# Output sums of an older attention head inside the next key strip, norm roots read from PSUM, and a later release of weight strips 2 and 3

## Chip, cores and metric

The kernel runs on one core of one Trainium2 chip. The metric is the device time of one execution in microseconds, as the median of the runs. An engine is named by its role: TensorE (PE in the profile, PEld for its weight loads), VectorE (DVE), ScalarE (ACT), GpSimd (POOL), SyncE (SP).

## What is computed

Two diffusion blocks in a row on 256 latent tokens (x) and 256 context tokens (ctx) of width 2048, batch 1, all in fp32. Each block has two layers. A layer first normalizes both streams and modulates them with vectors that come from the conditions c and c_ctx, runs a mixer, and adds the gated result.

```python
h_lat = rms_norm(x, norm_g[i]) * (1.0 + scale[:, None]) + shift[:, None]
h_ctx = rms_norm(ctx, norm_g[i]) * (1.0 + cscale) + cshift
# block 1, layer 0: gated linear recurrence (rglru_mixer), both streams
# block 1, layer 1: differential attention, 16 heads of 2 x 64, latent queries, 512 keys
attn = p[:, :, 0] - lam * p[:, :, 1]          # two softmaxes per head
o = rms_norm(o, subln_g) * (1.0 - lam_init)   # over the 128 output features of a head
y_lat = (o * jax.nn.silu(g)) @ w_out
# block 2, layers 0 and 1: chunked SGU and grouped-query attention
x = x + gate[:, None] * y_lat
```

## The kernel before

**Layout and strips.** Activations lie with features on the 128 partitions, 16 tiles of 128 features, with 256 latent and 256 context tokens in the free dimension (512 together). Every projection is cut into strips: a strip is 128 output columns of a weight matrix, 128 x 2048, streamed from HBM in two halves of 512 KB. To keep fp32 precision at the fast matmul rate, weights and activations are split in a high and a low part (type fp32r). ScalarE writes the high part `w_hi` (`split_hi`, L223) and VectorE the rest `w_lo` (`split_lo`, L231), always one pair of strips ahead. TensorE makes three matmuls per feature tile (`strip`, L249 to L251), so a strip has two halves of 24 matmuls; `between(half)` is called after each half. SyncE issues the strip loads (`load_strip`, L215) and waits before each for the split of the strip two before it. Strips 0 and 1 are loaded at once, the loop over the other pairs begins behind a wait for `mod_used`, which counts products of modulation chunks (L1979).

**The start.** `start_pe` computes the first 8 groups of modulation columns. A group is four chunks of 1 MB, each multiplied with the conditions (`mod_products`, L299, 8 instructions as counted in the profile). GpSimd issues the chunk loads, chunk q of a group as soon as chunk q of the group before has been used (L1807). `mod_turn` (L322) turns a group's rows into columns, VectorE adds the bias and modulates four feature tiles, and TensorE runs the tiles of strips 0 and 1 that are ready (`first_tiles`, L288 to L290). The tiles 8 to 15 follow behind group 7.

**The norms.** `norm_pe` sums the squares into bank 6 (L484), ScalarE takes the root (L499), VectorE the reciprocal (L507), and TensorE broadcasts it over the partitions into the same bank (L493, semaphore `rstd_ps`). ScalarE copies it to SBUF (L503, `rstd_done`). VectorE, which in between has split half a strip, then multiplies tile by tile (`context`, L541 and L543), ScalarE adds the shift and writes the high part (L522), VectorE writes the low part (L550), and TensorE starts the tile in the next projection. There are four norms; the one in the start (layer 0) uses the copy in its own code.

**The attention.** `att_pe`, `att_act` and `att_dve` run one body per head i, in an order written by hand. `here` is the projection of head i: four strips, key (c = 0, 512 columns), query (1, 256), value (2, 512) and gate (3, 256). `before` is the attention of head i - 1, `older` the norm of the output of head i - 2. The queues of the engines are in order, with semaphores of one count per head between them. TensorE's body is: key strip, modulation chunk, scores of the head before (L1099), sum of squares of the older output (L1104, into bank 6, `M_BANK`), query strip, sum of squares of the keys (L1114, `M_BANK`), value strip, modulation chunk, sum of squares of the queries (L1118, `M_BANK`), transposes of the attention weights, gate strip, output product, value transposes. ScalarE copies and squares the keys (L1165, L1166), splits, takes the four exponentials (L1174), the root of the older sums (L1178), copies and squares the queries (L1183, L1184), splits, takes the root of the key sums (L1187), copies the values (L1191), and so on, with a tanh for the gate (L1207) and, at the end, the copy and square of the output (L1216, L1217, `o_evac`) and the copy of the turned values (L1223). VectorE uses the older root in `root()` (L1258 on) and the exponentials in `weights()` (L1268 to L1272). The sum, root and wait for an older head stand beside a head's own projection in the heads 2 to 15. The wait in question on TensorE is:

```python
                    pe.wait_ge(A["k_evac"], i + 1)
                    if older:
                        pe.wait_ge(A["sdo"], i - 1)
                    if before:
                        pe.wait_ge(A["sdq"], i)
                    pe.matmul(psum[:, M_BANK, :], ones64, ksq, start=True, stop=True).then_inc(A["ssk"], 1)
```

Of the kernel before, what the change touches and what calls it, by code (L numbers as in the profile page):

```python
# [22 lines left out]
ALU = mybir.AluOpType  # L23
ACT = mybir.ActivationFunctionType
AX_X = mybir.AxisListType.X

P = 128
D = 2048
KT = D // P
T = 256  # L30
NT = 2 * T
# [5 lines left out]
HEADS1 = 16  # L37
# [46 lines left out]
def build(nc, ins, out):  # L84
    with ExitStack() as ctx:
# [411 lines left out]
        def norm_sqrt(act, l):  # L497
            act.wait_ge(S["ss_done"], l + 1)
            act.activation(rcol, psum[:, SS_BANK, 0:NT // P], ACT.Sqrt, scale=1.0 / D, bias=eps_col).then_inc(S["sd_done"], 1)  # L499
            if l > 0:  # L500
                split_hi(act, layer_strip[l] // 2, 1, halves=(0,))
            act.wait_ge(S["rstd_ps"], l + 1)
            act.activation(nb["rstd"], psum[:, SS_BANK, :], ACT.Copy).then_inc(S["rstd_done"], 1)  # L503

# [25 lines left out]
        def norm_dve(dve, l):  # L530
# [4 lines left out]
            dve.wait_ge(S["unit_cols"], UNITS_READY[l])  # L535
            dve.wait_ge(S["rstd_done"], l + 1)
            dve.wait_ge(S["strip_done"], layer_strip[l])

            def context(k, c):
                dve.wait_ge(S["h_ready"], KT * l + k - 3)  # L540
                dve.scalar_tensor_tensor(out=hs4[c][:, 0:T], in0=xl[:, k, :], scalar=mod_a[:, bass.ds(k, 1), 0],  # L541
                                         in1=nb["rstd"][:, 0:T], op0=ALU.mult, op1=ALU.mult)
                dve.scalar_tensor_tensor(out=hs4[c][:, T:NT], in0=y[:, 1, k, :], scalar=mod_a[:, bass.ds(k, 1), 1],  # L543
                                         in1=nb["rstd"][:, T:NT], op0=ALU.mult, op1=ALU.mult).then_inc(S["hf_done"], 1)

# [472 lines left out]
        def att_strip(j, par, c):  # L1018
            return Strip(S_ATT, 4 * par + c, j, 8)
# [54 lines left out]
        def att_pe(pe):  # L1074
            def body(j, par):
# [3 lines left out]
                def chunk(n):  # L1079
                    return lambda half: mod_chunk(pe, M_ATT + j, 2 * par + n) if half else None  # L1080
                first = isinstance(i, int) and i == 0
                last, end = (isinstance(i, int) and i == HEADS1 + n for n in range(2))
                if first:
                    first_pair(pe, S_ATT, [(psum[:, K_BANK, :], NT), (psum[:, Q_BANK, 0:T], T)], KT, 0, KT)
                    chunk(0)(1)
                elif here:
                    ge(pe, A["v_evac"], i)
                    strip(pe, att_strip(j, par, 0), psum[:, K_BANK, :], NT, chunk(0))
                if before:
# [6 lines left out]
                    for qt in range(2):  # L1096
# [4 lines left out]
                        mm.then_inc(A["scores"], 1)  # L1101
                if older:
                    pe.wait_ge(A["o_evac"], i - 1)
                    pe.matmul(psum[:, M_BANK, 0:T], ones, osq, start=True, stop=True).then_inc(A["sso"], 1)  # L1104
                if here:
# [48 lines left out]
        def att_act(act):  # L1154
            def body(j, par):
# [3 lines left out]
                if last:  # L1159
                    to_high(act, 1, 0, 6)  # L1160
                if here:
                    st = att_strip(j, par, 0)
# [5 lines left out]
                if before:  # L1168
                    ge(act, A["attn_t"], 2 * (i - 1))
                    for qt in range(2):  # L1170
                        act.wait_ge(A["negmax"], 2 * (i - 1) + qt + 1)
                        for c in range(2):
                            n = 2 * qt + c
                            act.activation(p1[qt][c], psum[:, S_BANK + n, :], ACT.Exp, bias=nm1[:, n:n + 1],  # L1174
                                           accum_out=rs1[:, n:n + 1]).then_inc(A["expd"], 1)
                if older:
                    act.wait_ge(A["sso"], i - 1)
                    act.activation(osq, psum[:, M_BANK, 0:T], ACT.Sqrt, scale=1.0 / P, bias=eps_col).then_inc(A["sdo"], 1)  # L1178
                if here:
# [791 lines left out]
        def _(sp):  # L1971
# [4 lines left out]
            for par in range(2):  # L1976
                load_strip(sp, 0, par, True)
            sp.wait_ge(S["mod_used"], 4 * (MOD_FIRST - 2))
            with sp.Fori(1, N_STRIPS // 2) as pair:  # L1979
# [199 lines left out]
```

## Time and profile before

| | us |
|---|---|
| Median of 3 runs | 2805.18 (2803.17 to 2805.68) |
| Profiled execution, time | 2805.79 |
| Profiled execution, span | 2804.1 |
| TensorE busy in the span | 2639.0 |
| VectorE busy | 2045.8 |
| ScalarE busy | 1224.6 |

The span is what the profiler saw of one execution; the device time holds 1.7 us more around it. A busy time is the sum over an engine's instructions. Matmuls are pipelined, so the interval between two starts is shorter than the duration of one, and this text counts with starts.

### The profile page before, as it was taken

The numbers are of one execution on the slowest core, as the hardware profiler recorded it, in microseconds if no ns is written. First come the engines' busy times: TensorE is split into PE (matmuls) and PEld (weight loads), VectorE is DVE, ScalarE is ACT, GpSimd is POOL, SyncE is SP. The second block draws the span as 40 slices with busy tenths as digits, with TensorE's granted clock in tenths as the row PEclk, the third lists the DMA queues.
The fourth block names the chain that finished last, engine by engine and source line by source line (L and its number), as shares of the span: only waits on it lengthen the run. The fifth ranks groups of instructions, "written<-read, shape, count | busy, mean of one in ns | idle before, by whom it ended". The sixth has DMA issues, their size and how long they took to land.

```text
span 2804.1 us, 39539 instructions
## 1 busy us (share of the span) xinstructions
PE 2639.0 (94%) x13490; PEld 2133.3 (76%) x13490; DVE 2045.8 (73%) x3196; ACT 1224.6 (44%) x1875; POOL 211.6 (8%) x402
## 2 busy tenths in 40 slices
PE   5799999999899999999989899999998997999989
PEld 1477777788677777777768788888886887998978
DVE  4399999999778788687877777764454666775655
ACT  3266556622443444444345433323444324544642
POOL 1110011011000000000000011100000100110000
PEclk8799999999999999999999899999999998999999
DMA  9765455476455565565655355532221643873325
GB/s 370 287 196 164 166 181 177 145 262 225 180 180 204 178 199 181 183 209 195 217 187 193 131 188 182 187 123 99 68 74 49 223 148 124 282 239 120 122 101 167
DMA packets 126557, 498.35 MB, mean 178 GB/s; under 512 B 14464, under 2 KB 16512, under 8 KB 116608
## 3 DMA queue, kind: packets, MB, share of 16 engines
q1 hardware_dynamic: 74176, 267.49, 27.7%
q0 software_dynamic: 52288, 229.66, 23.8%
q8 instruction: 53, 0.87, 0.1%
q14 instruction: 40, 0.33, 0.0%
HBM read 492.90 MB, written 4.19 MB: 177 GB/s over the span
## 4 chain that ended last, share of the span: by engine, by line
PE 75%; DVE 12%; issue 5%; DMA 4%; ACT 3%; DVEq 1%; POOL 0%; ACTq 0%; POOLq 0%; SPq 0%
PE psum L249 18%; PE psum L251 18%; PE psum L250 18%; PE psum L262 4%; DMA y<-in_mod_weights 2%; DVE w_lo L231 2%; PE psum L263 2%; DVE psum L409 2%; PE psum L299 2%; ACT w_hi L223 1%; PE psum L1631 1%; PE psum L1099 1%; PE psum L836 1%; DVE work L411 1%; PE psum L1645 1%
## 5 line engine op out<-in xcount | busy, mean ns | idle before, releaser
L249 PE MATMUL psum<-h_both,w_hi 128*128 128x512 f32 (+1 forms) x3264 | 1184.3, 363 | 5.6 <-DVE w_lo L231 5.6
L251 PE MATMUL psum<-h_both,w_lo 128*128 128x512 f32 (+1 forms) x3264 | 1156.1, 354 | 0.0
L250 PE MATMUL psum<-h_both,w_hi 128*128 128x512 f32 (+1 forms) x3264 | 1155.4, 354 | 0.0
L231 DVE TENSOR_TENSOR w_lo<-raw,w_hi 128x1024 fp32r<-128x1024 f32 x496 | 584.9, 1220 | 305.3 <-ACT w_hi L223 302.4
L249 PEld LDWEIGHTS psum<-h_both,w_hi 128*128 128x128 f32 x3264 | 619.6, 190 | 100.0 <-issue 13.2
L250 PEld LDWEIGHTS psum<-h_both,w_hi 128*128 128x128 f32 x3264 | 619.8, 190 | 92.4 <-issue 9.8
L251 PEld LDWEIGHTS psum<-h_both,w_lo 128*128 128x128 f32 x3264 | 619.1, 190 | 85.8
L223 ACT ACTIVATE w_hi<-raw 128x1024 fp32r<-128x1024 f32 x496 | 496.7, 1052 | 388.3 <-PE psum L251 301.4
L262 PE MATMUL psum<-h_both,w_hi 128*128 128x512 f32 x480 | 177.0, 409 | 10.0 <-DVE h_both L609 9.6
L263 PE MATMUL psum<-h_both,w_lo 128*128 128x256 f32 x480 | 137.0, 286 | 0.0
L409 DVE SCALAR_TENSOR_TENSOR psum<-y,modraw 128x1024 f32<-128x1024 f32 x98 | 120.3, 1228 | 21.1 <-DMA y<-in_mod_units 18.5
L411 DVE SCALAR_TENSOR_TENSOR y<-y,modraw 128x1024 f32<-128x1024 f32 x98 | 119.5, 1220 | 0.0
L262 PEld LDWEIGHTS psum<-h_both,w_hi 128*128 128x128 f32 x480 | 92.6, 193 | 34.2 <-issue 6.2
L263 PEld LDWEIGHTS psum<-h_both,w_lo 128*128 128x128 f32 x480 | 93.1, 194 | 1.5
L409 DVE SCALAR_TENSOR_TENSOR psum<-work,modraw 128x1024 f32<-128x1024 f32 x62 | 76.1, 1227 | 2.4 <-DMA work<-in_mod_units 2.4
L411 DVE SCALAR_TENSOR_TENSOR work<-work,modraw 128x1024 f32<-128x1024 f32 x62 | 75.6, 1220 | 0.0
L1165 ACT ACTIVATE y<-psum 128x512 f32<-128x512 f32 x16 | 9.6, 597 | 148.8 <-PE psum L251 146.8
L288 PE MATMUL psum<-h_both,w_hi 128*128 128x512 f32 (+1 forms) x128 | 54.9, 429 | 20.6 <-DVE h_both L550 16.8
L1191 ACT ACTIVATE y<-psum 128x512 f32<-128x512 f32 x16 | 9.6, 597 | 143.6 <-PE psum L251 143.6
L299 PE MATMUL psum<-modraw,cond 128*32 128x512 f32 x384 | 60.0, 711 | 12.2 <-DMA modraw<-in_mod_weights 8.6
L836 PE MATMUL psum<-work 128*128 128x512 f32 x128 | 59.0, 604 | 6.9 <-DVE work L931 6.6
L757 DVE SCALAR_TENSOR_TENSOR y<-psum,mod,work 128x256 f32<-128x256 f32 x32 | 15.4, 483 | 67.0 <-PE psum L251 57.8
(289 smaller groups left out, 3127.3 us busy)
## 6 DMA issues: line engine op xcount, KB each, us to landing
raw<-in_weights SPq DMA_DIRECT2D x496, 512.0 KB, 4.4
y<-in_mod_units POOLq DMA_DIRECT2D x130, 512.0 KB, 4.2
modraw<-in_mod_weights POOLq DMA_DIRECT2D x48, 1024.0 KB, 5.5
work<-in_mod_units POOLq DMA_DIRECT2D x62, 512.0 KB, 4.6
y<-in_mod_weights POOLq DMA_DIRECT2D x16, 1024.0 KB, 9.1
xl<-in_mod_units POOLq DMA_DIRECT2D x32, 512.0 KB, 4.8
modraw<-in_mod_units POOLq DMA_DIRECT2D x32, 512.0 KB, 4.7
modraw<-in_cond_rows POOLq DMA_DIRECT2D x6, 1024.0 KB, 8.0
```

What stands on the lines that cost most here:

```text
L223: act.activation(w_hi[:, par, half, :], raw[:, 2 * par + half, :], ACT.Copy).then_inc(S["split_hi"], 1)
L231: dve.tensor_tensor(w_lo[:, par, half, :], raw[:, 2 * par + half, :], w_hi[:, par, half, :].bitcast(F32), ALU.subtract).then_inc(S["split_ ...
L249: pe.matmul(dst, hi, h_hi[:, k, 0:n], start=(k == 0), stop=False)
L250: pe.matmul(dst, hi, h_lo[:, k, 0:n], start=False, stop=False)
L251: mm = pe.matmul(dst, lo, h_hi[:, k, 0:n], start=False, stop=(k == KT - 1))
L262: pe.matmul(joined, hi, h_both[:, :, k, 0:T], start=(k == 0), stop=False)
L263: return pe.matmul(bank[:, 0:T], lo, h_hi[:, k, 0:T], start=False, stop=False)
L288: pe.matmul(dst, hi, h_hi[:, k, 0:n], start=(k == 0), stop=False)
L299: mm = pe.matmul(bank[32 * j:32 * j + 32, :], cond[:, 4 * q + j, :], chunk[:, j, :], start=(q == 0), stop=(q == 3))
L409: dve.scalar_tensor_tensor(out=out, in0=mw[:, half, :], scalar=0.5, in1=rows[:, 0, part], op0=ALU.mult, op1=ALU.mult, accum_out=macc[:, pa ...
L411: dve.scalar_tensor_tensor(out=mw[:, half, :], in0=mw[:, half, :], scalar=0.5, in1=rows[:, 1, part], op0=ALU.mult, op1=ALU.mult, accum_out ...
L836: pe.matmul(psum[:, GATE_BANK + g, :], lw["gw"][par][:, g, :], lw["xc"], start=True, stop=True).then_inc(L["gate_done"], 1)
```

## The change

In the attention, for heads that have their own projection, the sum of squares of the older output moves from behind the scores to between the halves of the key strip (`sums`, called by `key_strip`). TensorE waits there for the older output's squares (`o_evac`) and for the root of the queries (`sdq`). ScalarE takes the older root ahead of its key copy and then runs one Exp on one column (`warm`). The last two bodies, which have no projection of their own, stay as they were. In the norms of layers 1 to 3 the copy of the root to SBUF goes, and VectorE waits for TensorE's `rstd_ps` and reads bank 6. SyncE waits for 28 products, not 24, before the loads of strips 2 and on.

```diff
--- before.py
+++ after.py
@@ -499,8 +499,9 @@
             act.activation(rcol, psum[:, SS_BANK, 0:NT // P], ACT.Sqrt, scale=1.0 / D, bias=eps_col).then_inc(S["sd_done"], 1)
             if l > 0:
                 split_hi(act, layer_strip[l] // 2, 1, halves=(0,))
-            act.wait_ge(S["rstd_ps"], l + 1)
-            act.activation(nb["rstd"], psum[:, SS_BANK, :], ACT.Copy).then_inc(S["rstd_done"], 1)
+            else:
+                act.wait_ge(S["rstd_ps"], 1)
+                act.activation(nb["rstd"], psum[:, SS_BANK, :], ACT.Copy).then_inc(S["rstd_done"], 1)
 
         def norm_reciprocal(dve, l):
             dve.wait_ge(S["sd_done"], l + 1)
@@ -533,15 +534,15 @@
             dve.wait_ge(S["mod_a_done"], MOD_FIRST // 2 + l)
             dve.wait_ge(S["mod_cols"], MODS_READY[l])
             dve.wait_ge(S["unit_cols"], UNITS_READY[l])
-            dve.wait_ge(S["rstd_done"], l + 1)
+            dve.wait_ge(S["rstd_ps"], l + 1)
             dve.wait_ge(S["strip_done"], layer_strip[l])
 
             def context(k, c):
                 dve.wait_ge(S["h_ready"], KT * l + k - 3)
                 dve.scalar_tensor_tensor(out=hs4[c][:, 0:T], in0=xl[:, k, :], scalar=mod_a[:, bass.ds(k, 1), 0],
-                                         in1=nb["rstd"][:, 0:T], op0=ALU.mult, op1=ALU.mult)
+                                         in1=psum[:, SS_BANK, 0:T], op0=ALU.mult, op1=ALU.mult)
                 dve.scalar_tensor_tensor(out=hs4[c][:, T:NT], in0=y[:, 1, k, :], scalar=mod_a[:, bass.ds(k, 1), 1],
-                                         in1=nb["rstd"][:, T:NT], op0=ALU.mult, op1=ALU.mult).then_inc(S["hf_done"], 1)
+                                         in1=psum[:, SS_BANK, T:NT], op0=ALU.mult, op1=ALU.mult).then_inc(S["hf_done"], 1)
 
             def low(k, c):
                 dve.wait_ge(S["hhi_done"], KT * l + k + 1)
@@ -1078,6 +1079,17 @@
 
                 def chunk(n):
                     return lambda half: mod_chunk(pe, M_ATT + j, 2 * par + n) if half else None
+
+                def sums():
+                    pe.wait_ge(A["o_evac"], i - 1)
+                    pe.wait_ge(A["sdq"], min(i, HEADS1) if isinstance(i, int) else i)
+                    pe.matmul(psum[:, M_BANK, 0:T], ones, osq, start=True, stop=True).then_inc(A["sso"], 1)
+
+                def key_strip(half):
+                    if half:
+                        mod_chunk(pe, M_ATT + j, 2 * par)
+                    elif older:
+                        sums()
                 first = isinstance(i, int) and i == 0
                 last, end = (isinstance(i, int) and i == HEADS1 + n for n in range(2))
                 if first:
@@ -1085,7 +1097,7 @@
                     chunk(0)(1)
                 elif here:
                     ge(pe, A["v_evac"], i)
-                    strip(pe, att_strip(j, par, 0), psum[:, K_BANK, :], NT, chunk(0))
+                    strip(pe, att_strip(j, par, 0), psum[:, K_BANK, :], NT, key_strip)
                 if before:
 
                     pe.wait_ge(A["qr"], i)
@@ -1099,9 +1111,8 @@
                             mm = pe.matmul(psum[:, S_BANK + 2 * qt + c, :], qr[rows, qt * P:(qt + 1) * P], kr[rows, :],
                                            start=True, stop=True)
                         mm.then_inc(A["scores"], 1)
-                if older:
-                    pe.wait_ge(A["o_evac"], i - 1)
-                    pe.matmul(psum[:, M_BANK, 0:T], ones, osq, start=True, stop=True).then_inc(A["sso"], 1)
+                if older and not here:
+                    sums()
                 if here:
                     if not first:
                         pe.wait_ge(A["sgl"], i)
@@ -1158,6 +1169,13 @@
                 last = isinstance(i, int) and i == HEADS1
                 if last:
                     to_high(act, 1, 0, 6)
+
+                def root():
+                    act.wait_ge(A["sso"], i - 1)
+                    act.activation(osq, psum[:, M_BANK, 0:T], ACT.Sqrt, scale=1.0 / P, bias=eps_col).then_inc(A["sdo"], 1)
+                if older and here:
+                    root()
+                    act.activation(warm, eps_col, ACT.Exp)
                 if here:
                     st = att_strip(j, par, 0)
                     act.wait_ge(S["strip_done"], st.s + 1)
@@ -1173,9 +1191,8 @@
                             n = 2 * qt + c
                             act.activation(p1[qt][c], psum[:, S_BANK + n, :], ACT.Exp, bias=nm1[:, n:n + 1],
                                            accum_out=rs1[:, n:n + 1]).then_inc(A["expd"], 1)
-                if older:
-                    act.wait_ge(A["sso"], i - 1)
-                    act.activation(osq, psum[:, M_BANK, 0:T], ACT.Sqrt, scale=1.0 / P, bias=eps_col).then_inc(A["sdo"], 1)
+                if older and not here:
+                    root()
                 if here:
                     st = att_strip(j, par, 1)
                     act.wait_ge(S["strip_done"], st.s + 1)
@@ -1975,7 +1992,7 @@
             sp.dma_start(consts[:, :], ins["consts"]).then_inc(S["consts_in"], 16)
             for par in range(2):
                 load_strip(sp, 0, par, True)
-            sp.wait_ge(S["mod_used"], 4 * (MOD_FIRST - 2))
+            sp.wait_ge(S["mod_used"], 4 * (MOD_FIRST - 1))
             with sp.Fori(1, N_STRIPS // 2) as pair:
                 for par in range(2):
                     load_strip(sp, pair, par)
```

## Rows read from the trace of the kernel before

**Rows 1.** The page, busy time, share and instructions of each engine over the span

```profile
PE 2639.0 (94%) x13490; PEld 2133.3 (76%) x13490; DVE 2045.8 (73%) x3196; ACT 1224.6 (44%) x1875; POOL 211.6 (8%) x402
```

**Rows 2.** TensorE's waits, whole span: total us, times, longest us

```profile
PE psum L1114 <- issue: 18.6, 14, 1.4
```

**Rows 3.** Timeline of TensorE, head 4: start us, us, what, idle before

```profile
921.76 0.28 PE L251 MATMUL psum<-h_both,w_lo 128*128 128x256 f32 x1
923.37 1.10 PE L1114 MATMUL psum<-y,consts 128*128 128x512 f32 x2 [1.34 <-issue]
...
924.76 0.40 PE L251 MATMUL psum<-h_both,w_lo 128*128 128x512 f32 x1
```

**Rows 4.** Timeline of ScalarE, head 4: from the key copy to the root

```profile
912.79 0.60 ACT L1165 ACTIVATE y<-psum 128x512 f32<-128x512 f32 x1 [11.15 <-PE psum L251]
...
921.50 1.28 ACT L1178 ACT_TABLE_LOAD   x1
922.80 0.47 ACT L1178 ACTIVATE work<-psum,small 128x256 f32<-128x256 f32 x1
```

**Rows 5.** Timeline of TensorE, head 1, the stretch of rows 3

```profile
787.71 0.28 PE L251 MATMUL psum<-h_both,w_lo 128*128 128x256 f32 x1
...
789.14 0.40 PE L251 MATMUL psum<-h_both,w_lo 128*128 128x512 f32 x1
```

**Rows 6.** Timeline of TensorE, scores to query strip, heads 1 and 2

```profile
780.06 1.99 PE L1099 MATMUL psum<-y,work 64*128 64x512 f32 x8
...
782.32 0.28 PE L251 MATMUL psum<-h_both,w_lo 128*128 128x256 f32 x1
...
823.87 1.99 PE L1099 MATMUL psum<-y,work 64*128 64x512 f32 x8
...
826.56 0.28 PE L251 MATMUL psum<-h_both,w_lo 128*128 128x256 f32 x1
```

**Rows 7.** Timeline of VectorE, head 4, its use of the root

```profile
923.30 1.75 DVE L1258 RECIPROCAL work<-work 128x256 f32<-128x256 f32 x1 [3.37 <-ACT work L1178]
```

**Rows 8.** Timelines of VectorE and ScalarE in the three later norms

```profile
717.47 0.48 DVE L541 SCALAR_TENSOR_TENSOR work<-xl,small,work 128x256 f32<-128x256 f32 x1 [0.41 <-ACT work L503]
717.87 0.48 DVE L543 SCALAR_TENSOR_TENSOR work<-y,small,work 128x256 f32<-128x256 f32 x1
...
1559.35 0.60 ACT L503 ACTIVATE work<-psum 128x512 f32<-128x512 f32 x1 [1.43 <-PE psum L493]
...
1560.24 0.48 DVE L541 SCALAR_TENSOR_TENSOR work<-xl,small,work 128x256 f32<-128x256 f32 x1 [1.07 <-ACT work L503]
...
2334.21 0.48 DVE L541 SCALAR_TENSOR_TENSOR work<-xl,small,work 128x256 f32<-128x256 f32 x1 [0.15 <-issue]
```

**Rows 9.** Groups of VectorE by line: busy us, mean ns, idle before

```profile
L541 DVE SCALAR_TENSOR_TENSOR work<-xl,small,work 128x256 f32<-128x256 f32 x48 | 23.0, 479 | 1.6 <-ACT work L503 1.5 <-issue 0.2
...
L757 DVE SCALAR_TENSOR_TENSOR y<-psum,mod,work 128x256 f32<-128x256 f32 x32 | 15.4, 483 | 67.0 <-PE psum L251 57.8 <-DMA work<-in_ctx_t 5.3 <-PE psum L627 3.7
```

**Rows 10.** Timeline of VectorE, a residual update of both streams

```profile
711.77 0.48 DVE L757 SCALAR_TENSOR_TENSOR y<-psum,mod,work 128x256 f32<-128x256 f32 x1 [5.92 <-PE psum L251]
712.17 0.47 DVE L763 SCALAR_TENSOR_TENSOR xl<-psum,mod,work 128x256 f32<-128x256 f32 x1
```

**Rows 11.** Timelines of SyncE and TensorE in the start

```profile
94.23 2.20 SPq L215 DMA_DIRECT2D raw<-in_weights  x4
...
104.97 1.06 PE L299 MATMUL psum<-y,cond 128*32 128x512 f32 x8 [1.87 <-DMA y<-in_mod_weights]
...
118.66 1.93 PE L299 MATMUL psum<-y,cond 128*32 128x512 f32 x8 [0.36 <-DMA y<-in_mod_weights]
```

**Rows 12.** DMA queues, packets, MB, share: 100 to 110, then 110 to 120

```profile
q0 software_dynamic: 333, 2.43, 58.5%
q1 hardware_dynamic: 491, 1.75, 43.8%
...
q0 software_dynamic: 390, 2.80, 67.4%
```

## Prediction

> **What bounds the kernel now.** I read the page first, for the span and the share of each engine. The profiled execution took 2805.79 us, of which the span is 2804.1; TensorE is busy for 94% of it [rows 1]. So a step counts if TensorE waits for it, and the second view is the list of TensorE's waits. Its largest entry inside the loops is the matmul of L1114, the sum of squares of a head's keys: 14 waits, 18.6 us in all, 1.4 us at most [rows 2]. The view names "issue", that is, it found no releaser, so I went to the timelines of one head (i = 4). Its query strip issues its last matmul at 921.76, the next matmul, L1114, starts at 923.37, and the third matmul of the value strip (the first L251) is at 924.76 [rows 3]. ScalarE tells why. After the four exponentials it loads a table at 921.50, takes the root of the output sums of the head two back (L1178) at 922.80, and goes on with the query copy when the root ends at about 923.2 [rows 4]. L1111 makes TensorE wait for that root before it overwrites M_BANK. The wait follows the root closely in time, and it occurs in just the 14 heads that have an older head beside them (i = 2 to 15).
>
> **Part 1, the attention.** What goes: the wait. In head 1, which has no older head, the stretch from the last query matmul to the first L251 of the value strip lasts 787.71 to 789.14, 1.43 us [rows 5]; in head 4 it lasts 921.76 to 924.76, 3.00 us [rows 3]. The difference is 1.57 us, by 14 heads 22.0 us. (The waits' view says 18.6, since it takes modelled ends of matmuls; I use starts.)
>
> What moves: one matmul of 256 columns in two passes per head. Removing it from behind the scores saves: head 1 takes 780.06 to 782.32 from its first scores matmul to the first L251 of the query strip, 2.26 us; the same stretch with the sums takes 823.87 to 826.56, 2.69 us [rows 6]. So 0.43 us per head are saved there. Putting it into the key strip costs an unknown amount, because there it cuts a run of fast matmuls in two, which no row shows for 256 columns. The bounds: not less than the same 0.43 us; not more than what L1114, twice as wide, adds between two strips. That stretch of 1.43 us would be 0.12 + 0.23 + 0.22 = 0.57 us by the pitches of the strips alone (0.12 us at 256 columns, 0.23 at 512), so L1114 costs 0.86 us [rows 5]. L1114 is itself such a cut, so I take its 0.86 less half of its two passes (about 0.2 us, half of the 0.43), some 0.65, and 0.08 for the two waits that now stand inside a strip. Net cost (0.73 - 0.43) x 14 = 4.2 us, bounds 0 and (0.86 - 0.43) x 14 = 6.0 us.
>
> The new waits: TensorE waits in the middle of the key strip for the squares of the older output (L1217) and for the earlier root of the queries. ScalarE has done L1217 and the copy behind it before it idles 11.15 us up to its key copy at 912.79 [rows 4], and the middle of the strip (24 matmuls of 0.23 us from its end) is about 5.5 us before that copy. So L1217 has some 5 us of slack, and the root of the queries, a value strip older, more. On the other side the root now stands ahead of the key copy on ScalarE: root 0.47, a table load of 1.28 back to the exponential set, and the one-column Exp (no row shows one; less than the 256 columns of the root), about 2.2 us after the sums, with some 5 us to go. The first load, to the root's set, can run while ScalarE waits, as no work precedes it. What is queued behind the root is the key copy, its weight split and the exponentials; the exponentials lose their table load of 1.28 us and the root, and the load comes back ahead of L1187 (root of the key sums). The query copy, which now waits for ScalarE until 923.2, can start when its strip ends, 0.3 us after its last start at 921.76, so some 1.2 us earlier; with the load of 1.28 us L1187 ends where it ends now, and TensorE wants it only after the value strip (48 matmuls of 0.23 us, 11 us). On VectorE the 3.37 us that it waited ahead of L1258 [rows 7] go, so the attention weights and the next splits come earlier. VectorE is the busiest other engine (73% of the span [rows 1]), but a head gets shorter by 1.3 us and VectorE sheds 3.37 us of waiting: it is no nearer to being the bound. With the stall gone nothing else is late in a head except 0.7 us in each odd head for the modulation row, which stays. Part 1: -22.0 + 4.2 = -17.8 us, from -22 to -16.
>
> **Part 2, the norms.** The copy of the root to SBUF goes in three norms (the first keeps it). VectorE waited for it 0.41, 1.07 and 0.15 us [rows 8]. The first and the third go entirely, since TensorE is done by then and VectorE's own weight split ends last. In the second norm the copy itself starts at 1559.35, so TensorE is done at that time and VectorE could start there instead of at 1560.24: 0.85 us. Sum 1.4 us; VectorE then paces the norm tile by tile and TensorE waits for each tile, so all of it passes on. Added: 96 multiplications read their second operand from PSUM. The nearest rows are the residual updates L757, also scalar_tensor_tensor on 128x256 with one operand in PSUM: 483 ns, against 479 ns of L541 from SBUF [rows 9], and two of either kind in a row start 0.40 us apart [rows 8, 10]. That makes 96 x 4 ns = 0.4 us at most; I take nothing. Part 2: -1.4 us, from -1.5 to +0.4.
> The Trainium skill speaks against this part. "VectorE: DVE Perf Modes" (the TRN2 errata table and the rules for kernel authors) gives VectorE's fixed term as 58 cycles from SBUF and 120 from PSUM, and advises a copy to SBUF where many operations read the same data. By it, as an estimate, each read would cost 62 cycles at its 0.96 GHz, 65 ns, and part 2 would come out at +4.8 instead of -1.4. The rows of this case, 483 against 479 ns, do not agree with it.
>
> **Part 3, the start.** SyncE issues the four half strips of pair 1 from 94.2 on [rows 11], after the products of six groups; after the change it does so behind those of seven, at about 104 (these now begin their last chunk at 104.97, having waited 1.87 us for it [rows 11]). Nothing else is passed in SyncE's queue, and the strips are wanted only after the first block, long after group 7. What changes is what they compete with: now the last chunks of group 6 and the first of group 7, then group 7 alone. From 100 to 110 the chunks get 2.43 MB and the strips 1.75 MB, 0.418 MB per us in all; from 110 on the chunks alone have 2.80 MB left, done by 110 + 6.7 = 116.7 [rows 12], and TensorE begins the last products of group 7 at 118.66 [rows 11]. After the change group 6 comes without the strips, some 2 us earlier, but only the end of group 7 is on the path. Its chunks can be issued when group 6 has freed their buffers, from 102 on, with the first bytes near 103.8, just when the strips are released. 4.2 MB of chunks and 2.1 MB of strips take 6.3 / 0.418 = 15.0 us: the transfers end at 118.8 if the strips win throughout, 2.1 us later than now. If the strips begin 2.5 us behind and take a third of the rate, the chunks are through at 103.8 + 2.5 + 3.15 / 0.28 = 117.6, and with a fifth at 115.7. The gain for group 6 is given back in group 7: between -1 and +2 us, and I take +0.7, near the middle.
>
> **Sum.** -17.8 - 1.4 + 0.7 = -18.5 us. On the profiled execution: 2805.79 - 18.5 = 2787.3. That execution lies 0.61 us above the median of the runs, 2805.18, so the time to expect is 2786.7 us.
>
> **Rivals.**
> A, PSUM operands are slow in the norms. Place: the 96 multiplications. Consecutive ones overlap now (0.48 us each, 0.40 us apart [rows 8]); if a read from PSUM ends the overlap, each costs 0.08 us: 96 x 0.08 = 7.7 us on top, 2794.4. Against it, L757 and the update behind it read PSUM and overlap just so [rows 10]; for it, only two of them stand in a row there, beside no splits of ScalarE. 9%. A sentence on the page of part 2: by the Trainium skill's figure ("VectorE: DVE Perf Modes", the errata table) the same rival would give 6.2 us and 2792.9.
> B, the stall's real releaser is another. The view says "issue", and ScalarE's query copy stands behind the root in any case. If TensorE waits at L1114 for something that the change does not move, only parts 2 and 3 and the move itself remain: -1.4 + 0.7 + 4.2 = +3.5, which is 2808.7, within 0.2%. Against it: the 14 heads are exactly those with an older head, and head 1 passes L1114 without a wait [rows 5]. 3%.
> C, slower: the cut in the key strip is dear. Place: between the two halves of 14 key strips, where two waits stop TensorE from loading its next weights ahead. It decides when one cut costs over 18.5 / 14 = 1.3 us more than I took, 2.1 us in all; to end 0.2% slower it must cost 2.5 us, giving 14 x 1.8 = 25 us on top, 2811.4. The dearest cut in the rows is 0.86 us. 2%.
> D, the gain of the wait is only partly kept: after it ScalarE or VectorE is late elsewhere in a head, for instance since two more table loads per head (28 in all, 1.28 us each, 36 us on ScalarE) push the root of the key sums or the splits. If half of the 22 us comes back: 2786.7 + 11 = 2797.7. ScalarE is idle for more than half of the attention, which speaks against it. 7%.
> E, the start is better or worse than I hold it, and TensorE's clock there falls and rises at other times. Such an end costs or gives up to 3 us and stays within the range.
>
> **How the numbers follow.** The forecast has 79%. Its own bounds are -22 - 1.5 - 1 = -24.5 (2780.7) and -16 + 0.4 + 2 = -13.6 (2791.6). With part of A, and a little for the clock of the start, the range goes from 2779.5 to 2794.0. A measurement of this kernel can tell about 0.2%, 5.6 us, from no change. Faster by more than that (below 2799.6): forecast, A, D, 95%. Within: B, 3%. Slower: C, 2%.
>
> **What would show it.** Right: L1114 gone from TensorE's waits; the stretch from the last query matmul to the first L251 at about 1.4 us in every head; every head shorter by 1.2 to 1.3 us; L1104 in the middle of the key strip and the L249 behind it some 0.7 us later than the pitch; two more table loads per head; L541 and L543 at 480 ns each and the same pace; the last products of group 7 between 117.5 and 121. Wrong: L1114 still preceded by idle time (B), a key strip longer by 2 us (C), a new entry of over 0.5 us per head among TensorE's waits (D), L541 and L543 starting 0.48 us apart (A). The prediction as a whole would be wrong if heads shorten by less than 1 us each.

## The result, and the profile after

| | before | after | ratio, 95% interval |
|---|---|---|---|
| first comparison, median of 4 runs each | 2805.36 us | 2779.43 us | 0.991 [0.9893, 0.9928] |
| the same kernels again, with the parts (23 and 6 runs) | 2803.54 us | 2782.86 us | 0.9922 [0.991, 0.9935] |
| and again, on another chip (15 and 5 runs) | 2803.59 us | 2779.08 us | 0.9913 [0.990, 0.9927] |

The change makes the kernel faster by 25.9, 20.7 and 24.5 us in the three comparisons; 18.5 us were forecast, for 2786.7 us. The first median lies 0.07 us below the low end of the range, 2779.5, the second inside, the third 0.4 us below. The sign and the cause were right and the size was too small. Two runs in the slow state, 4401 us with the attention alone and 11967 us with the start alone, are in no time or ratio of this text.

The page of the changed kernel, its span and the busy times that answer [rows 1]. TensorE is busy for 4.4 us less and idle for some 20 us less; ScalarE is busy for 40 us more, of which 35.9 are 28 more table loads of 1.28 us.

```profile
span 2780.1 us, 39603 instructions
...
PE 2634.6 (95%) x13490; PEld 2128.9 (77%) x13490; DVE 2044.9 (74%) x3196; ACT 1264.4 (45%) x1914; POOL 212.5 (8%) x402
```

The timeline of TensorE in head 4 of the changed kernel, the stretch of [rows 3]; L1125 is the old L1114. It no longer waits: the third matmul of the value strip follows the last of the query strip by 919.27 - 917.83 = 1.44 us, where it was 3.00, and as head 1 did in [rows 5]. In the list of TensorE's waits L1125 has no row.

```profile
917.83 0.28 PE L251 MATMUL psum<-h_both,w_lo 128*128 128x256 f32 x1
917.95 1.02 PE L1125 MATMUL psum<-y,consts 128*128 128x512 f32 x2
...
919.27 0.40 PE L251 MATMUL psum<-h_both,w_lo 128*128 128x512 f32 x1
```

The timeline of TensorE in the middle of the same head's key strip, where the sums now stand (L1086). From the last matmul of the first half to the third of the second it takes 904.07 - 902.96 = 1.11 us; three pitches of 0.23 would be 0.68. So the sums cost 0.43 us there, exactly what [rows 6] showed for the old place.

```profile
902.96 0.39 PE L251 MATMUL psum<-h_both,w_lo 128*128 128x512 f32 x1
903.18 0.59 PE L1086 MATMUL psum<-work,consts 128*128 128x256 f32 x2
...
904.07 0.40 PE L251 MATMUL psum<-h_both,w_lo 128*128 128x512 f32 x1
```

The timeline of ScalarE in that head, which answers [rows 4]. The root's table is loaded at 897.72, during the idle time; the root (L1175) waits 4.81 us for the sums, the load back and the one-column Exp are done by 905.8, and the key copy still waits 3.49 us for TensorE. After the exponentials ScalarE idles for 0.15 us and takes the query copy 0.32 us behind the start of the strip's last matmul.

```profile
897.72 1.28 ACT L1175 ACT_TABLE_LOAD   x1
903.82 0.47 ACT L1175 ACTIVATE work<-psum,small 128x256 f32<-128x256 f32 x1 [4.81 <-PE psum L1086]
904.31 1.28 ACT L1178 ACT_TABLE_LOAD   x1
905.60 0.20 ACT L1178 ACTIVATE small<-small 128x1 f32<-128x1 f32 x1
909.30 0.60 ACT L1183 ACTIVATE y<-psum 128x512 f32<-128x512 f32 x1 [3.49 <-PE psum L251]
...
918.15 0.39 ACT L1200 ACTIVATE work<-psum 128x256 f32<-128x256 f32 x1 [0.15 <-PE psum L251]
```

The timeline of VectorE in the second of the three norms, and in the second fence the instructions of L542 (ns minimum, median, maximum), for [rows 8, 9]. The multiplication starts 1.14 us behind the start of the weight split, without the 1.07 us of idle time of before; it takes 476 ns with the operand in PSUM, 479 before, and the next starts 0.39 us later.

```profile
1533.46 1.23 DVE L231 TENSOR_TENSOR w_lo<-raw,w_hi 128x1024 fp32r<-128x1024 f32 x1 [0.76 <-ACT w_hi L223]
1534.60 0.47 DVE L542 SCALAR_TENSOR_TENSOR work<-xl,small,psum 128x256 f32<-128x256 f32 x1
1534.99 0.47 DVE L544 SCALAR_TENSOR_TENSOR work<-y,small,psum 128x256 f32<-128x256 f32 x1
```

```profile
L542 DVE SCALAR_TENSOR_TENSOR work<-xl,small,psum x48: 472/476/480, 716.7 to 2333.9; 128x256 f32<-128x256 f32 x48
```

The broadcast in that norm (L493, timeline of TensorE), before and, in the second fence, changed. It took 2.07 us in one execution, at a granted clock of 0.50, and 1.16 in the other, at 1.00, though nothing of it was changed, so part of the 1.07 us went by the clock and not by the edit (more of this at the norms alone).

```profile
1557.24 2.07 PE L493 MATMUL psum<-consts,small 128*128 128x128 f32 x8 [0.63 <-DVE small L507]
```

```profile
1532.75 1.16 PE L493 MATMUL psum<-consts,small 128*128 128x128 f32 x8 [0.63 <-DVE small L508]
```

The timelines of SyncE and TensorE in the start, for [rows 11]. The strips go out at 103.43 instead of 94.23. The last chunk of group 6 no longer keeps TensorE waiting, but each of the last two chunks of group 7 does for 1.8 us, and the last products start at 118.45, where it was 118.66.

```profile
103.43 46.63 SPq L215 DMA_DIRECT2D raw<-in_weights  x7
```

```profile
101.12 1.90 PE L299 MATMUL psum<-y,cond 128*32 128x512 f32 x16
...
114.71 1.93 PE L299 MATMUL psum<-y,cond 128*32 128x512 f32 x8 [1.83 <-DMA y<-in_mod_weights]
118.45 1.93 PE L299 MATMUL psum<-y,cond 128*32 128x512 f32 x8 [1.81 <-DMA y<-in_mod_weights]
```

**Where the time went.** Matching TensorE's matmuls of the two profiled executions by their number in the program, the changed one is ahead by 0.2 us at the last chunk of group 7, by 0.4 at the end of the recurrence (680 us), by 0.9 at the end of the first norm's tiles (743), by 0.85 before head 2's key sums and by 22.3 at 1435, when the heads with an older head are over. So 21.5 us come from the heads. Of the remaining 2.5 us to 24.0 (2804.1 to 2780.1), 3.3 are gained around the second norm, 2.8 are lost at 2110 to 2158 us, and the rest is pieces under 2 us. The first of these goes with the clock (below), and so does the second: the mean granted clock in that stretch was 0.96 before and 0.90 after.

### The profile page after: what moved, and what is told of

It is laid out like the page before. It is cut to its first block, busy times and chain, and to the rows that moved or that the text cites. A ratio compares the mean times of both kernels' runs of the same rounds, so it can differ in the third digit from the quotient of the medians.

```text
span 2780.1 us, 39603 instructions
## 1 busy us (share of the span) xinstructions
PE 2634.6 (95%) x13490; PEld 2128.9 (77%) x13490; DVE 2044.9 (74%) x3196; ACT 1264.4 (45%) x1914; POOL 212.5 (8%) x402
## 3 DMA queue, kind: packets, MB, share of 16 engines
q1 hardware_dynamic: 74176, 267.49, 28.1%
## 4 chain that ended last, share of the span: by engine, by line
PE 78%; DVE 10%; issue 4%; DMA 4%; ACT 4%; DVEq 1%; POOL 0%; ACTq 0%; POOLq 0%; SPq 0%
PE psum L249 20%; PE psum L251 20%; PE psum L250 20%; PE psum L262 4%; DMA y<-in_mod_weights 2%; PE psum L263 2%; PE psum L299 2%; DVE w_lo L231 2%; PE psum L837 1%; DVE psum L409 1%; ACT w_hi L223 1%; PE psum L1648 1%; PE psum L1111 1%; DVE h_both L551 1%; PE psum L1662 1%
## 5 line engine op out<-in xcount | busy, mean ns | idle before, releaser
L409 DVE SCALAR_TENSOR_TENSOR psum<-y,modraw 128x1024 f32<-128x1024 f32 x98 | 120.4, 1229 | 19.8 <-DMA y<-in_mod_units 17.3
L263 PEld LDWEIGHTS psum<-h_both,w_lo 128*128 128x128 f32 x480 | 92.4, 193 | 1.4
L1208 ACT ACTIVATE y<-psum 128x512 f32<-128x512 f32 x16 | 9.6, 597 | 117.0 <-PE psum L251 117.0
L523 ACT ACTIVATE h_both<-work,mod 128x256 f32 (+1 forms) x96 | 43.3, 501 | 36.9 <-DVE work L544 36.9
```

Source lines behind the costliest of these rows:

```text
L263: return pe.matmul(bank[:, 0:T], lo, h_hi[:, k, 0:T], start=False, stop=False)
L409: dve.scalar_tensor_tensor(out=out, in0=mw[:, half, :], scalar=0.5, in1=rows[:, 0, part], op0=ALU.mult, op1=ALU.mult, accum_out=macc[:, pa ...
```

## Experiments

The theory is that the 14 waits behind the late root are the whole gain of the attention, that the norms give little over 1 us, and that the start gives nothing. The rival is that the surplus over the forecast comes from the start or the norms. A measure without the noise of whole runs is the interval between the key sums of heads 2k and 2k + 2 in the profile. It was 89.8 us before and is 86.7 after, and in each kernel all its values from head 2 on agree within 0.15 us.

**The attention alone.** The hunks of the attention put on the kernel before.

```diff
-                    strip(pe, att_strip(j, par, 0), psum[:, K_BANK, :], NT, chunk(0))
+                    strip(pe, att_strip(j, par, 0), psum[:, K_BANK, :], NT, key_strip)
...
+                if older and here:
+                    root()
+                    act.activation(warm, eps_col, ACT.Exp)
```

> The attention part alone on the kernel before. Theory 1: the wait of 1.57 us goes in 14 heads and the cut in the key strip costs exactly what the old place cost, as the trace of the changed kernel suggests (0.43 us either way): -22 us. The prediction as written: -17.8 us. Rival (the surplus of the whole change over the forecast comes from the start or the norms): this part alone gives only -17 to -19 us.

Measured: 2782.89 us against 2803.54, -20.7, ratio 0.9922 [0.9907, 0.9936]. Two heads take 86.73 us; from the key sums of head 2 to those of head 15 it is 562.8 us, where it was 582.6. That is 19.8 us over 13 heads, 1.52 each, and with head 2 itself 21.3. The whole change has the same 562.7. The part carries nearly all of the gain. The interval of the ratio goes from -26 to -18 us, so the times alone do not decide between theory 1 (-22) and the rival (-17 to -19); the 21.3 us of the trace do, for theory 1.

**The norms alone.**

```diff
-            act.wait_ge(S["rstd_ps"], l + 1)
-            act.activation(nb["rstd"], psum[:, SS_BANK, :], ACT.Copy).then_inc(S["rstd_done"], 1)
+            else:
+                act.wait_ge(S["rstd_ps"], 1)
+                act.activation(nb["rstd"], psum[:, SS_BANK, :], ACT.Copy).then_inc(S["rstd_done"], 1)
...
-                                         in1=nb["rstd"][:, 0:T], op0=ALU.mult, op1=ALU.mult)
+                                         in1=psum[:, SS_BANK, 0:T], op0=ALU.mult, op1=ALU.mult)
```

> The norm part alone on the kernel before. Theory 1: -1.4 us (0.41 + 0.85 + 0.15). Rival (the surplus lies here, since a norm that starts earlier meets other clock stretches): -3 to -5 us. Rival A of the prediction, slow reads from PSUM: +6 us.

Measured: 2802.71 against 2803.54 us, ratio 0.9992 [0.9981, 1.0003]: not to be told from no change, and rival A, +6 us, is out. In the profile the stretch of the first norm is 0.6 us shorter than before (60.1 for 60.7 us). In the second norm VectorE still waits, now for the broadcast:

```profile
1556.21 1.23 DVE L231 TENSOR_TENSOR w_lo<-raw,w_hi 128x1024 fp32r<-128x1024 f32 x1 [0.76 <-ACT w_hi L223]
1557.88 0.48 DVE L542 SCALAR_TENSOR_TENSOR work<-xl,small,psum 128x256 f32<-128x256 f32 x1 [0.44 <-PE psum L493]
```

The broadcast took 2.07 us here, as before. So like can be compared with like: from the start of the weight split to the first multiplication it is 1.67 us, where it was 2.30, when the broadcast takes 2.07 us; where it takes 1.16 us it is 1.14, where the kernels with the copy have 1.38. With 0.11 us more over the 16 tiles, a norm gains 0.74 us in the one case and 0.35 in the other, and three norms 1.0 to 2.2 us.

**The start alone.**

```diff
-            sp.wait_ge(S["mod_used"], 4 * (MOD_FIRST - 2))
+            sp.wait_ge(S["mod_used"], 4 * (MOD_FIRST - 1))
```

> The start part alone on the kernel before. Theory 1: +0.7 us, between -1 and +2, since what group 6 gains group 7 gives back. Rival (the surplus lies here): -3 to -5 us.

Measured: 2803.02 against 2803.54 us, -0.5, ratio 1.000 [0.9986, 1.0014]. In the trace the last products of group 5 and of group 7 start at 92.4 and 119.3, 27.0 us apart. The kernels that wait for six groups have 25.9 (before), 26.3 and 26.0 us there; those that wait for seven 27.0, 26.6, 28.1, 26.3, 27.1, 27.0 and 27.2. The mean goes from 26.0 to 27.0: the part costs 1 us of the path up to there. It does not end there. From the same products of group 5 to the end of the recurrence it takes 587.2 to 587.6 us in the three kernels with six groups and 587.5 to 592.8 in the seven with seven, 2.6 us more in the mean. What adds to the 1.0 us was not tested. The rival is out by these traces; the times by themselves tell only 4 us either way.

**The whole change again.**

> The whole change again beside its parts. Theory 1: -22 - 1.4 + 0.7 = -22.7 us, and what is beyond this is the clock of the stages, which moves with the time of day of each stage and adds or takes up to 3 us. If the parts add up to the whole within 1 us, no part depends on another.

Measured: -20.7 us, and the parts add up to -20.7 - 0.8 - 0.5 = -22.0, 1.3 us from the whole. Each of these differences is known to 3 to 4 us, so no part is seen to depend on another, and a dependence of a few us is not excluded.

**The cost of the cut.** The matmul of the sums twice in the key strip.

```diff
                     pe.wait_ge(A["sdq"], min(i, HEADS1) if isinstance(i, int) else i)
+                    if here:
+                        pe.matmul(psum[:, M_BANK, 0:T], ones, osq, start=True, stop=True)
                     pe.matmul(psum[:, M_BANK, 0:T], ones, osq, start=True, stop=True).then_inc(A["sso"], 1)
```

> The changed kernel with the matmul of the older head's sums run twice in the middle of the key strip (14 heads). Theory 1 (the matmul costs its two passes of 0.215 us each and the cut itself nothing): 0.43 us per head, two heads 86.7 + 0.86 = 87.6 us, +6 us. Rival (the prediction's reading, in which the passes are 0.2 us in all and the rest is the cost of leaving and entering the strip): 0.2 us per head, 87.1 us for two heads, +3 us.

The timeline of TensorE in that kernel, and two key sums two heads apart:

```profile
820.50 0.39 PE L251 MATMUL psum<-h_both,w_lo 128*128 128x512 f32 x1
820.73 0.59 PE L1087 MATMUL psum<-work,consts 128*128 128x256 f32 x2
821.16 0.59 PE L1088 MATMUL psum<-work,consts 128*128 128x256 f32 x2
...
822.05 0.40 PE L251 MATMUL psum<-h_both,w_lo 128*128 128x512 f32 x1
...
835.93 1.02 PE L1127 MATMUL psum<-y,consts 128*128 128x512 f32 x2
...
923.51 1.02 PE L1127 MATMUL psum<-y,consts 128*128 128x512 f32 x2
```

The second one starts 0.43 us behind the first, and the strip's third matmul comes 1.55 us after the last of the first half, 0.44 more than with one. Two heads take 87.58 us, 0.87 more. Time 2789.50 us, 0.9952 [0.9937, 0.9966]; the whole change was 2782.86 and 2779.08 in other comparisons. So one such matmul costs 0.43 us wherever it stands, and the cut itself costs nothing that a row shows. Theory 1 holds, and the reading in the prediction falls.

**Only the root's place on ScalarE.** TensorE's order of before, with the sums behind the scores, and the root ahead of the exponentials.

```diff
                     next_strip(split_hi, act, st)
+                    if older:
+                        root()
+                        act.activation(warm, eps_col, ACT.Exp)
                 if before:
                     ge(act, A["attn_t"], 2 * (i - 1))
```

> The changed kernel with TensorE's order of before (the sums of the older head behind the scores, no cut in the key strip), and ScalarE taking the root between the key split and the exponentials, followed by the one-column Exp. Theory 1 (only the root's place on ScalarE counts): ScalarE idles 2.9 us there for the maxima, the root and the load back take 0.5 + 1.3 + 0.2, the root's own load runs right behind the split; the wait at the key sums is gone, two heads take 86.7 us as in the changed kernel (89.8 before), time within 2 us of the changed kernel. Rival (the sums have to be early): the exponentials are delayed by over 0.5 us and with them the query copy, and part of the wait comes back, 87.5 us or more for two heads, +5 us or more.

The timeline of ScalarE in head 4 of that kernel, and in the second fence of TensorE at the key sums (L1123):

```profile
918.30 1.28 ACT L1173 ACT_TABLE_LOAD   x1
919.60 0.47 ACT L1173 ACTIVATE work<-psum,small 128x256 f32<-128x256 f32 x1
920.09 1.28 ACT L1183 ACT_TABLE_LOAD   x1
921.38 0.20 ACT L1183 ACTIVATE small<-small 128x1 f32<-128x1 f32 x1
921.49 0.67 ACT L1190 ACTIVATE y<-psum,small 128x512 f32<-128x512 f32 x1
...
924.59 0.39 ACT L1198 ACTIVATE work<-psum 128x256 f32<-128x256 f32 x1 [0.33 <-PE psum L251]
```

```profile
924.27 0.28 PE L251 MATMUL psum<-h_both,w_lo 128*128 128x256 f32 x1
924.39 1.02 PE L1123 MATMUL psum<-y,consts 128*128 128x512 f32 x2
```

The root fits into the time in which ScalarE waited for the maxima, it is done over 4 us before TensorE comes to the key sums, and there is no wait. Two heads take 86.6 us, 0.1 less than with the sums in the key strip. Time 2782.73 us, 0.9931 [0.9915, 0.9946]. Moving the sums on TensorE was not needed: the releaser that the waits' view called "issue" was the root standing behind four exponentials. This also settles rival B.

**Without the one-column Exp.**

```diff
                     root()
-                    act.activation(warm, eps_col, ACT.Exp)
```

> The changed kernel without the one-column Exp behind the early root. Theory 1: the table load then stands ahead of the first exponential, where ScalarE idles 2.9 us for the maxima; two heads stay at 86.7 us and the time within 1 us. Rival (the load is issued only when the maxima are there): exponentials 1.3 us later, the query copy late, a wait of up to 1.3 us at the key sums, up to +18 us.

The timelines of ScalarE and, in the second fence, of TensorE in head 4:

```profile
916.26 1.28 ACT L1191 ACT_TABLE_LOAD   x1 [2.92 <-DVE small L1270]
917.55 0.69 ACT L1191 ACTIVATE y<-psum,small 128x512 f32<-128x512 f32 x1
...
920.22 0.39 ACT L1199 ACTIVATE work<-psum 128x256 f32<-128x256 f32 x1
```

```profile
918.90 0.28 PE L251 MATMUL psum<-h_both,w_lo 128*128 128x256 f32 x1
919.02 1.02 PE L1125 MATMUL psum<-y,consts 128*128 128x512 f32 x2
```

The timeline of ScalarE in head 10 of the same kernel:

```profile
1171.51 2.00 ACT L223 ACTIVATE w_hi<-raw 128x1024 fp32r<-128x1024 f32 x2
1173.53 1.28 ACT L1191 ACT_TABLE_LOAD   x1
1176.39 0.69 ACT L1191 ACTIVATE y<-psum,small 128x512 f32<-128x512 f32 x1 [1.57 <-DVE small L1270]
```

Both were wrong in a point. In the heads 2 to 9 the load did come only when the maxima were there, against theory 1, so the exponentials start 1.3 us later and the query copy 1.32 us behind the start of its strip's last matmul, not 0.32. In the heads 10 to 15 the load runs right behind the split, as theory 1 had it, and costs nothing. In all 14 TensorE takes the key sums 0.12 us behind the query strip's last start, since they wait for the key copy and two roots, not for the query copy. Two heads take 86.7 us; time 2781.14, 0.9918 [0.9901, 0.9936]. The preload buys nothing here that a time or a head shows.

**The release behind eight groups.** First in the changed kernel (the diff), then alone on the kernel before.

```diff
-            sp.wait_ge(S["mod_used"], 4 * (MOD_FIRST - 1))
+            sp.wait_ge(S["mod_used"], 4 * MOD_FIRST)
```

> The changed kernel with strips 2 and 3 released after all eight groups, 32 products. Theory 1 (the strips are what delays group 7): the last products of group 7 start at about 115.3 instead of 118.5, and the rows of conditions and the strips, now issued together at about 117.5, still land before they are wanted (131 and 138): about -3 us at the first block, as far as the clock doesn't take it. Rival (given back once more): the rows of conditions land late, the chain of the first block moves by the same 3 us, 0 us.

> The kernel before with nothing but the release of strips 2 and 3 behind all eight groups. Theory 1 (strips and group 7 share the transfer rate, and the later release keeps them apart): from the first chunk load of group 7 to its last products 13.7 us (16.6 before, 16.0 and 17.3 where seven groups were waited for), the first block 2.5 to 3 us earlier. Time: -3 us, less than the runs can tell for certain. Rival: the first blocks of the recurrence wait for the strips, and the gain is gone by the second block.

The last products of group 7 in the changed kernel with eight groups, and the packets of the DMA queues from 104 to 118 us, first with seven (the changed kernel), then with eight:

```profile
114.51 1.06 PE L299 MATMUL psum<-y,cond 128*32 128x512 f32 x8 [1.00 <-DMA y<-in_mod_weights]
116.98 1.07 PE L299 MATMUL psum<-y,cond 128*32 128x512 f32 x8 [1.40 <-DMA y<-in_mod_weights]
```

```profile
q0 software_dynamic: 527, 3.79, 65.2%
q1 hardware_dynamic: 547, 2.03, 35.5%
```

```profile
q0 software_dynamic: 576, 4.19, 76.0%
```

With eight groups no strip moves while group 7 does. From its first load to its last products it takes 13.7 us in each of the three kernels that have it, 15.1 to 17.0 with six and 16.0 to 17.3 with seven. From the last products of group 5 it is 23.0 us, 3.0 less than with six and 4.0 less than with seven. The strips are still in time. To the end of the recurrence it is 583.2 to 584.4 us, 3.4 less than with six, so the lead is kept so far. The runs: 2778.89 us, 0.9913 [0.990, 0.9926], for the changed kernel with it; 2801.78 against 2803.59 us, 0.9990 [0.9981, 0.9999], alone, which is -1.8 us with an interval from -5.3 to -0.3. The traces fit theory 1, and they speak for delaying the transfer by two groups and not by one; as a time of the whole kernel the 3 us are not shown, and the changed kernel without it was not run beside the first.

**Both better variants together, and the whole change a third time.**

> The two better variants together: sums behind the scores with the root ahead of the exponentials, and strips 2 and 3 released behind eight groups. Theory 1: two heads take 86.6 us and group 7 takes 13.7 us, so 0.6 us from the heads and some 3 us from the start against the whole change: about 2778. Rival (the clock and the transfers of the later stages take it back): the same time as the whole change within 1 us.

> The whole change once more, beside the two others on one chip. Theory 1: -21 to -23 us against the kernel before; two heads 86.7 us. Rival (the -25.9 us of the first comparison is the true size): -25 us or more.

Measured: 2778.71 us, 0.9908 [0.9893, 0.9923], and 2779.08 us, 0.9913 [0.990, 0.9927], on one chip. Two heads take 86.64 and 86.7 us; group 7 takes 13.7 and 17.0 us. They are 0.4 us apart, as the rival had it. In the profiled executions the variant is 4.2 us ahead at the last products of group 7, 5.3 at the end of the recurrence and at the end of the heads, 2.9 behind the second norm, 1.3 at 2150 us and 1.2 at the end: the lead is lost behind the heads. Part of that is the clock: from 1400 to 1600 us its mean was 0.91 in the variant and 0.94 in the whole change. The whole change itself came out at -24.5 us, between theory 1 (-21 to -23) and the rival (-25 or more), so this run decides neither way.

**Why the comparisons differ by 5 us.** The stretch of TensorE's matmuls around the second norm took 63.2 us in the kernel before, 63.3 with the attention alone, 60.2 with the start alone, which both leave the norms as they are, and 62.7 in the last variant, whose norms are changed. The busy times by stretches, with TensorE's granted clock behind them, in the kernel before and, in the second fence, with the start alone:

```profile
1549.00:1613.00 64.00, 56.29 (x236) 44.60 (x235) 50.85 (x99) 29.74 (x52) 4.25 (x8) 0.87 0.39 128
```

```profile
1552.00:1613.00 61.00, 53.16 (x237) 41.03 (x236) 49.91 (x98) 30.38 (x53) 4.25 (x8) 0.94 0.39 129
```

The same work is done at a mean clock of 0.87 in one and 0.94 in the other: it spends less time at the lower of the two levels (1.2 and 2.4 GHz). Of the 3 us, 0.9 are VectorE's wait for the copy, 1.07 and 0.15 us, which was longer where the broadcast of L493 took 2.07 us and not 1.16. That is 3 us at one place, either way. The runs of the kernel before alone, on several chips, spread from 2796.3 to 2811.2 us. What shifts the stretches from run to run was not tested.

## Why the prediction came out as it did

**The bound.** Right. TensorE's wait at the key sums was the root of the older output, released late by ScalarE. The kernel with only the root's place on ScalarE changed in the attention shows it, and the one without the preload shows that the query copy, which moved with the root, is not what TensorE waits for.

**Part 1, -17.8 us, measured -21.4 in every trace with the change.** The 22.0 us for the wait were right to 0.5 us: 1.57 us in head 4, by 14. The term that failed is the net cost of the move, 4.2 us for 0.30 per head; it is zero, the lower bound that the prediction gave. The step was "0.86 less half of its two passes (about 0.2 us, half of the 0.43)". It read the two passes of L1114 as 0.43 us together and the rest as the price of leaving and entering a strip. But 0.43 us is one pass of 512 columns (the strip's next matmul comes 0.45 us behind the start of L1114, then waits for the second pass), so the whole 0.86 is passes, and 256 columns cost half of all of it, 0.43. The kernel with the sums taken twice measured just that. The row for the old place had said 0.43 us as well, and two rows in the ratio of their widths should have told that there is no fixed part. The 0.08 us for two waits inside a strip came from no row, and the runs show nothing for them. The slack was as worked out: the root waited 4.8 us for the sums, the key copy came without delay, L1204 ends at 922.7, and no other wait appeared in a head. Rival D did not occur, and of rival C nothing is seen.

**Part 2, -1.4 us.** Right in kind and, by the traces, in size (1.0 to 2.2 us), but too small to measure as a time. The waits of 0.41, 1.07 and 0.15 us are gone in the first profile of the changed kernel; in the second norm that is in part luck of the clock, since six of the nine kernels with the changed norms still wait 0.44 us there for the broadcast. The 0.85 us of the prediction for this norm is 0.63 where the broadcast takes as long. L542 takes 476 ns and the pairs keep their pace, so rival A is out. The Trainium skill's fixed term for a PSUM operand ("VectorE: DVE Perf Modes", the TRN2 errata table) would have made it 65 ns longer; the trace of the change shows 3 ns less than before. The copy to SBUF, one of the two ways that the Trainium skill gives for many operations on a matmul's output (the same page, the rules for kernel authors), gained nothing here: without it a norm is 0.35 to 0.74 us shorter.

**Part 3, +0.7 us.** Right in sign, and in size up to the end of group 7: the traces show 1.0 us more from group 5 to group 7. At the end of the recurrence it is 2.6 us in the mean (0.2 to 5.4), which the prediction's bound of +2 did not foresee; the times show neither. The trade was as described, group 6 early and group 7 late. What was not worked out is that one more group would have separated the two.

**The sum.** With the cut at zero the same working gives -22.7 us, and the three comparisons, -25.9, -20.7 and -24.5, have a mean of -23.7, and -22.7 lies inside the interval of each. So of the 7.4 us that the first comparison had over the forecast, 4.2 are the cut and 3.2 are of the size by which the comparisons differ among themselves; the range had left too little for these.

## What to carry to other kernels

When an engine waits for a small result that another engine makes late, look at what stands ahead of it in that engine's queue, and at where that engine idles earlier: here 1.5 us per head went by moving one root ahead of four exponentials. Price an inserted instruction by two rows of different width before giving it a fixed part. When a load is delayed so that it doesn't disturb a critical one, see which later load it lands on: one step further may be free of both, as the traces here show up to the end of the recurrence.

## What the hardware showed beyond expectation

At the full clock a plain fp32 matmul of 256 columns costs TensorE 0.43 us in two passes of 0.215, and 512 columns 0.86, against 0.12 and 0.23 us for one fp32r matmul of the strips. Put between two of these it costs its passes and nothing more.

A table load does not always run ahead of the wait of its activation. For the root in the key strip it came 6 us early, during the idle time; for the first exponential without the preload it came after the wait for the maxima in eight heads, and before it in six. What divides them can be read from the trace: in the eight, a waiting instruction of its own (EVENT_SEMAPHORE of L1188, 17 ns, the first at 829.5 us) stands directly ahead of the load; in the six the work before does. In the changed kernel 103 of the 163 loads stand directly behind work, and each of them starts within 0.02 us of its end, though 63 of their activations then wait; the 24 loads with idle time ahead of them all have an instruction of the sequencer in front.

While strips and chunks moved together, from 104 to 118 us, the chunks got 3.79 MB and the strips 2.03 MB, and TensorE waited 1.8 us for each of the last two chunks.
